# A ring of eight gathered rows beside the attention heads, and the buffers that make room for it

## The reference, cut to what matters

```
def peer_block(xb):                                   # 128 frames
    q = (xb @ w_pq).reshape(t, PEER_HEADS, 2, PEER_HALF)
    s = einsum('thpd,phkd->thpk', q, sub_keys)        # 2 x 128 scores, 8 heads
    top_s, top_i = top_k(s, 16)
    best_s, best_j = top_k(all 256 sums, 16)          # 16 experts per frame and head
    g = softmax(best_s)
    h = einsum('td,thkd->thk', xb, u_emb[expert])
    act = g * gelu(h)
    return einsum('thk,thkd->td', act, v_emb[expert])
x = x + peer(rms_norm(x, g_ffn));  y = rms_norm(x, g_final)
```

## Time and profile before

| what | value |
|---|---|
| median of 3 runs | 3593.12 us (3592.84 to 3595.46) |
| the profiled execution's own time | 3593.41 us |
| its span, first to last instruction | 3591.7 us |
| granted TensorE clock, mean | 0.848 |
| first gather issued | 484.85 us |
| last gather issued | 3564.17 us |

### The profile page before, as it was taken

The page is one execution under the profiler, slowest core; times in us unless marked ns, Lnnn a source line. Parts: engine busy times, 40 slices in busy tenths (PEclk is TensorE's granted clock), DMA queues, the critical chain, the costliest instruction groups (busy, mean ns, idle before and its releaser), DMA issues. The chain is left out here.

```text
span 3591.7 us, 41643 instructions
## 1 busy us (share of the span) xinstructions
PE 2535.7 (71%) x13407; PEld 1076.0 (30%) x13407; DVE 2442.1 (68%) x6857; ACT 1020.4 (28%) x2925; POOL 1418.8 (40%) x1266
## 2 busy tenths in 40 slices
PE   5999867666866677667666866687667666666654
PEld 3444533222322233223322332233223222222211
DVE  2888666667666666776667667666667666666774
ACT  2333322222222222222322222323332222222321
POOL 0332434434444443444434443434344434344443
PEclk9999889887888898888888988887888878888866
DMA  7112369999999999999999999999999999999997
GB/s 251 47 50 70 98 230 381 382 386 383 396 391 384 380 386 379 380 379 385 393 380 382 388 379 388 374 385 376 385 370 401 378 374 369 344 385 371 365 371 297
DMA packets 219401, 1220.43 MB, mean 340 GB/s; under 512 B 33091, under 2 KB 60419, under 8 KB 79942
## 3 DMA queue, kind: packets, MB, share of 16 engines
q0 software_dynamic: 156672, 1140.92, 81.4%
q1 hardware_dynamic: 62533, 77.09, 6.6%
HBM read 1199.51 MB, written 18.42 MB: 339 GB/s over the span
## 5 line engine op out<-in xcount | busy, mean ns | idle before, releaser
L1374 PE MATMUL ps<-uv_rows,diag 64*64 64x512 f32 x8704 | 1381.8, 761 | 967.7 <-ACT diag L1619 966.8
L1270 POOL DMA_INDIRECT uv_rows<-in_uv_emb,experts x1088 | 1255.6, 1154 | 1823.9 <-PE ps L1374 1536.1
L1832 DVE CUSTOM_DVE_ANT_0 uv_rows<-uv_rows,handed 128x1024 f32<-128x1024 f32 x1088 | 1331.9, 1224 | 862.6 <-DMA uv_rows<-in_uv_emb,experts 856.7
L1374 PEld LDWEIGHTS ps<-uv_rows,diag 64*64 64x64 f32 x8704 | 329.1, 157 | 1655.0 <-ACT diag L1619 1221.8
L1611 ACT ACTIVATE gelu_c<-dots 128x2 f32<-128x2 f32 x544 | 110.8, 204 | 1880.4 <-DVE dots L1832 1880.0
L1619 ACT ACTIVATE diag<-ident_twice,act_c 128x64 f32<-128x64 f32 x1088 | 319.1, 340 | 286.4 <-DVE act_c L1849 285.8
L1334 PE MATMUL ps<-w_pq_sb,xnT_c 128*128 128x256 f32 x1152 | 349.1, 434 | 0.7 <-ACT xnT_c L1580 0.7
L1334 PEld LDWEIGHTS ps<-w_pq_sb,xnT_c 128*128 128x128 f32 x1152 | 224.7, 212 | 260.6 <-issue 236.0
L568 PE MATMUL ps<-w_in_sb,w_out_sb 128*128 128x512 f32 (+1 forms) x656 | 243.3, 526 | 16.8 <-ACT w_out_sb L454 16.8
L626 DVE SCALAR_TENSOR_TENSOR handed<-w_out_sb,tapsT,handed 128x128 f32<-128x128 f32 x960 | 252.8, 343 | 0.0
L389 POOL TENSOR_TENSOR rstd_a<-ms_a,neg_half 128x1 f32<-128x1 f32 x9 | 82.5, 9166 | 205.2 <-ACT ms_a L435 205.2
(11 more groups left out here) (244 smaller groups left out, 2127.1 us busy)
## 6 DMA issues: line engine op xcount, KB each, us to landing
uv_rows<-in_uv_emb,experts POOLq DMA_INDIRECT x1088, 9.0
w_in_sb<-in_w_in SPq DMA_DIRECT2D x4, 2048.0 KB, 11.7
w_pq_sb<-in_w_pq SPq DMA_DIRECT2D x8, 1024.0 KB, 12.2
w_out_sb<-in_x_prompt SPq DMA_DIRECT2D x8, 512.0 KB, 3.9
handed<-in_x_prompt SPq DMA_DIRECT2D x8, 512.0 KB, 3.8
w_out_sb<-in_w_out SPq DMA_DIRECT2D x1, 4096.0 KB, 19.3
out<-handed SPq DMA_DIRECT2D x8, 512.0 KB, 9.3
keys_turned<-handed SPq DMA_DIRECT2D x10, 260.0 KB
```

Of the source, the lines that this page charges most:

```text
L1270: nc.gpsimd.indirect_dma_start(out=rows[:, m % RING, :], out_offset=None, in_=d.uv_emb[0], in_offset=bass.IndirectOffsetOnAxis(ap=experts[ ...
L1374: ins = pe.matmul(ps[dst, 2 * x + half, :], diag[src, (m + i) % DIAGS, :], rows[src, (m + i) % RING, cols], start=first, stop=last)
L1832: nc.vector.tensor_tensor_reduce(out=row, in0=row, in1=xn[:, block_of(n) % 2, :], scale=1.0, scalar=0.0, op0=ALU.mult, op1=ALU.add, accum_ ...
```

## The change

The ring has eight rows instead of six. Each row takes 8 KB in every partition, and these buffers are given up or made smaller for it:

- `DIAGS` is 6 instead of 8.
- `q` and `qT` share one buffer, so that ACT waits with the next query until the scores are made. `half_s` has one buffer for two, so that the copy of the scores waits until the choice before has read its own.
- `gf` is gone. `gm` holds the chunks of both gains, and a new `final_gains` makes the final gain in PSUM (bank `X_`, half by half, in steps 9 and 13 of a block's first item; for the sample frames in two banks after the last item). `normalise` works on halves, in steps 12 and 15, from PSUM. `y_ready` counts two for a block, and `store` and `project` wait for both.
- The sample frames' convolution `y_s` lives in phase B alone. SP stores it to HBM at that phase's end and waits for it. Phase C loads it as it loads that of the other blocks.
- `probsT` holds one piece of up to 512 keys for two. The values are weighed piece by piece (`weigh_head_values` in step 3 and step 5, `pv_piece` in place of `pv_psum`), and the second piece is copied out when the first was weighed. `q_pair` is the first 128 columns of `probsT`, so that the query rows are loaded after step 5 of the item before their use, and no longer two pairs ahead.
- `heads_o` is the first half of `catT`, from the third head on. The first two heads of a block go to a small buffer `first_o`, as `catT` is still read by the projection then. `z` shares `conv_in`. Nine small columns are one tile.

```
-        RING = 6
-        DIAGS = 8
+        RING = 8
+        DIAGS = 6
-        qT = sb("qT_c", [P, 2, P])
-        half_s = sb("half_scores", [P, 2, 2, s.NKEYS])
+        qT = q[:, :].rearrange("p (a t) -> p a t", a=2)
+        half_s = sb("half_scores", [P, 2, s.NKEYS])
-        gm = sb("g_ffn_chunks", [s.DCH, P])
-        gf = sb("g_final_rows", [P, s.D])
+        gm = sb("gain_chunks", [2 * s.DCH, P])
-        q_pair = sb("pair_queries", [P, 2 * s.HD])
-        probsT = sb("head_probsT", [P, 2, BANK])
-        heads_o = sb("head_outputs", [P, s.DA])
+        probsT = sb("head_probsT", [P, BANK])
+        q_pair = probsT[:, 0:2 * s.HD]
+        first_o = sb("first_outputs", [P, P])
+        heads_o = catT[:, 0:s.CCH, :].rearrange("p c t -> p (c t)")
...
-        z = sb("conv_rows", [P, s.DC])
+        z = conv_in[:, :, :].rearrange("p c t -> p (c t)")
...
 # phase B, SP, at its end
+            sp.wait_ge(taps_done, 1)
+            sp.dma_start(d.conv[s.NB, :, :, 0:s.TS], y_s[:, :, :]).then_inc(y_kept, 16)
+            sp.wait_ge(y_kept, 16)
...
 # phase C, SP
-                sp.wait_ge(y_ready, b + 1)
+                sp.wait_ge(y_ready, 2 * (b + 1))
...
-            sp.dma_start(gf[:, :], d.g_final.partition_broadcast(P)).then_inc(gains_here, 16)
+            sp.dma_start(gm[s.DCH:2 * s.DCH, :], d.g_final.rearrange("(c p) -> c p", p=P)).then_inc(gains_here, 16)
-            sp.wait_ge(qT_h_psum, 1)
-            load_query_rows(1)
             for n in range(HEADS):
                 if 2 <= n < ITEMS and n % 2 == 0:
-                    sp.wait_ge(pv_psum, n)
+                    sp.wait_ge(pv_piece, pieces_before(n))
                     load_values(n // 2)
+                if n % 2 == 1 and n + 1 < ITEMS:
+                    sp.wait_ge(pv_piece, pieces_before(n))
+                    load_query_rows((n + 1) // 2)
...
-                if n % 2 == 1 and (n + 1) // 2 + 1 < ITEMS // 2:
-                    sp.wait_ge(qT_h_psum, (n + 1) // 2 + 1)
-                    load_query_rows((n + 1) // 2 + 1)
...
 # phase C, PE: in project, i == 0
+                    if p > 1:
+                        pe.wait_ge(y_ready, 2 * (p - 1))
...
+            def final_gains(b, half):
+                pe.wait_ge(gains_here, 32)
+                if b < s.NB:
+                    pe.wait_ge(y_ready, 2 * b + half)
+                bank = X_ if b < s.NB else X_ + half
+                for x in range(4):
+                    row = s.DCH + 4 * half + x
+                    ins = pe.matmul(ps[:, bank, x * P:(x + 1) * P],
+                                    g.ident[0:2 * s.DCH, row:row + 1].broadcast_to([2 * s.DCH, P]), gm[:, :], start=True, stop=True)
+                ins.then_inc(final_psum, 1)
...
+            def weigh_head_values(i, piece):
+                lo, hi = pieces_of(i)[piece]
+                pe.wait_ge(turned_ready, pieces_before(i) + piece + 1)
...
+                for x in range(lo, hi, P):
+                    ins = pe.matmul(ps[:, S_, O_AT:O_AT + s.HD], probsT[:, x - lo:x - lo + P],
+                                    v_pair[:, x // P, (h % 2) * s.HD:(h % 2 + 1) * s.HD], start=(x == 0), stop=(last and x == hi - P))
+                ins.then_inc(pv_piece, 1)
...
                     if k == 3 and len(pieces_of(i)) == 2:
+                        weigh_head_values(i, 0)
                         turn_head_probs(i, 1)
...
+                    if n >= PH and n % PH == 0 and n <= PROMPT and k in (9, 13):
+                        final_gains(block_of(n) - 1, (k - 9) // 4)
...
 # phase C, ACT
+                if r > 0:
+                    act.wait_ge(s_psum, r)          # query_out
...
-                if r >= 2:
-                    act.wait_ge(s_used, r - 1)
+                if r > 0:
+                    act.wait_ge(s_used, r)          # scores_out
...
-                if i > 0:
-                    act.wait_ge(pv_psum, i)
+                if i > 0 or piece:
+                    act.wait_ge(pv_piece, pieces_before(i) + piece)   # head_probs_out
...
+                if h == 2:
+                    act.wait_ge(x1_psum, 2 * (i // s.H + 1))          # head_output
+                dst = first_o if h < 2 else heads_o
...
 # phase C, DVE
-            def normalise(b):
+            def normalise(b, half):
...
+                dve.wait_ge(final_psum, 2 * b + half + 1)
+                nc.vector.scalar_tensor_tensor(out=x1[0:r, b % 2, cols], in0=x1[0:r, b % 2, cols], scalar=rms[0:r, 2:3],
+                                               in1=ps[0:r, bank, :], op0=ALU.mult, op1=ALU.mult).then_inc(y_ready, 1)
```

More of the change, by code:

```diff
@@ L749, in tap @@
                                                    in1=c.tapsT[:, :, j:j + 1].broadcast_to([P, s.CCH, s.TS]), op=ALU.mult))
-                before = g.b_dw.unsqueeze(2).broadcast_to([P, s.CCH, s.TS]) if j == 0 else g.y_s[:, :, :]
-                ins = nc.gpsimd.tensor_tensor(out=g.y_s[:, :, :], in0=tapped[:, :, :], in1=before, op=ALU.add)
+                before = g.b_dw.unsqueeze(2).broadcast_to([P, s.CCH, s.TS]) if j == 0 else y_s[:, :, :]
+                ins = nc.gpsimd.tensor_tensor(out=y_s[:, :, :], in0=tapped[:, :, :], in1=before, op=ALU.add)
                 if j + 1 < s.TAPS:
@@ L1222, in load_query_rows @@
                 b, h = item_of(2 * pair)
-                sp.dma_start(q_pair[:, :], d.q[b, :, h * s.HD:(h + 2) * s.HD]).then_inc(q_here, 16)
+                sp.dma_start(q_pair, d.q[b, :, h * s.HD:(h + 2) * s.HD]).then_inc(q_here, 16)
             def load_conv(b):
-                sp.dma_start(conv_in[:, :, :], d.conv[b]).then_inc(conv_here, 16)
+                t = P if b < s.NB else s.TS
+                sp.dma_start(conv_in[:, :, 0:t], d.conv[b, :, :, 0:t]).then_inc(conv_here, 16)
             load_query_rows(0)
@@ L1422, in turn_conv @@
                 pe.wait_ge(piece_read, pieces_before(s.H * i + 3))
-                if b < s.NB:
-                    pe.wait_ge(conv_here, 16 * (i + 1))
+                pe.wait_ge(conv_here, 16 * (i + 1))
+                t = P if b < s.NB else s.TS
                 for x in range(s.CCH):
[L1426 to L1429, removed]
+                    ins = pe.transpose(ps[0:t, B_, x * P:(x + 1) * P], conv_in[:, x, 0:t], g.ident[:, :])
                 ins.then_inc(y_psum, 1)
@@ L1445, in turn_outputs @@
                 for x in range(s.CCH):
-                    ins = pe.transpose(ps[:, B_, x * P:(x + 1) * P], heads_o[:, x * P:(x + 1) * P], g.ident[:, :])
+                    ins = pe.transpose(ps[:, B_, x * P:(x + 1) * P], first_o[:, :] if x == 0 else heads_o[:, x * P:(x + 1) * P],
+                                       g.ident[:, :])
                 ins.then_inc(oT_psum, 1)
+            def final_gains(b, half):
[6 more added lines that the diff above has]
+                    ins = pe.matmul(ps[:, bank, x * P:(x + 1) * P],
+                                    g.ident[0:2 * s.DCH, row:row + 1].broadcast_to([2 * s.DCH, P]), gm[:, :], start=True, stop=True)
+                ins.then_inc(final_psum, 1)
             def head_scores(i, piece):
@@ L1492, in weigh_head_values @@
                 pe.wait_ge(s_out, issued.scores)
[L1493 to L1499, removed]
+                last = hi == keys_of(i)
+                if last:
+                    issued.values += 1
+                for x in range(lo, hi, P):
+                    ins = pe.matmul(ps[:, S_, O_AT:O_AT + s.HD], probsT[:, x - lo:x - lo + P],
+                                    v_pair[:, x // P, (h % 2) * s.HD:(h % 2 + 1) * s.HD], start=(x == 0), stop=(last and x == hi - P))
+                ins.then_inc(pv_piece, 1)
             def head_step(n, k):
@@ L1572, in _ @@
                             turn_query(routed[1])
+                    if n >= PH and n % PH == 0 and n <= PROMPT and k in (9, 13):
+                        final_gains(block_of(n) - 1, (k - 9) // 4)
                     head_step(n, k)
+            for half in range(2):
+                final_gains(s.NB, half)
         @block.scalar
@@ L1638, in conv_rows_out @@
                 act.wait_ge(y_psum, i + 1)
-                if i > 0:
-                    act.wait_ge(zT_psum, i)
                 own = slice(0, P if FIRST + i < s.NB else s.TS)
-                nc.scalar.copy(z[own, :], ps[own, B_, :]).then_inc(y_out, 1)
+                nc.scalar.copy(z[own], ps[own, B_, :]).then_inc(y_out, 1)
             def conv_scaled(i):
@@ L1658, in head_probs_out @@
                 act.wait_ge(turned_psum, pieces_before(i) + piece + 1)
-                if i > 0:
-                    act.wait_ge(pv_psum, i)
-                nc.scalar.copy(probsT[:, piece, 0:hi - lo], ps[:, B_, 0:hi - lo]).then_inc(turned_ready, 1)
+                if i > 0 or piece:
+                    act.wait_ge(pv_piece, pieces_before(i) + piece)
+                nc.scalar.copy(probsT[:, 0:hi - lo], ps[:, B_, 0:hi - lo]).then_inc(turned_ready, 1)
             def head_output(i):
                 _, h = item_of(i)
-                at = O_AT
```

(16 more changed lines are left out.)

38 lines of the change are left out of this document (15 added, 23 removed).

## The result

The changed kernel takes 3393.24 us (median of 4 runs, 3392.87 to 3393.65), the kernel before 3594.29 us beside it: the ratio is 0.9433, 95% interval 0.941 to 0.9455. That is 201 us less where 112 were forecast, and under the range of 3435 to 3565. The profiled execution of the changed kernel has a span of 3391.9 us.

The account below looks back on a forecast made before the run. The prediction took phase C to be bound by its gathers, with too few in the DMA at a time. From 3593.4 us it took 115 for the ring and added 2.7 and 0.2: 3481 us, range 3430 to 3534.

Parts of the forecast that it names:

- What bounds the kernel: Phase C runs at the pace of its gathered rows, in a loop of 17.4 us for six rows; depth is short.
- The ring's term: Two more ring rows in phase C raise 380 GB/s to 395 over 1155 MB: 115 us less.
- The burst: At the first gathers, six issued before one was used moved 426 and 433 GB/s; one or two out, 341.
- The third reading: 504 stretches of 5 us sorted by gathers out: 354 GB/s with 2, 390 with 3, 404 with 4.
- The part outside the DMA stays 8.0 us: Of a ring turn in phase C, 8.0 us stay outside the DMA, so both added rows go into it.
- The convolution's store: End of phase B: the new store stands behind POOL's last tap, 2.7 us on the path, between 2 and 5.
- Smaller diagonals: ACT's diagonals of a pair wait until PE has weighed the pair three before: no cost.
- The final gain: PE's added matmuls and DVE's half reads: hidden, 0.2 us on the path; 21 or 16 us if not covered.
- SP's queue: Query rows loaded after step 5 for step 15: 27 us against a landing of 6.8 that may grow by 5; nothing.
- The rival of the late small loads: The deeper queue delays SP's query rows past step 15, so PE waits; 3643 us at landings of 33 us; chance 0.05.
- Share only: Rival: the DMA's rate while busy doesn't rise, only its idle tenths go: 3550 us (3534 to 3575); chance 0.24.
- no gain: Rival: something that depth doesn't touch sets 380 GB/s, such as memory or POOL's descriptors: 3596 us; chance 0.06.

Follow-up runs that it names:

- e4: Kernel before, ring of six, PE weighing only the first half of the v columns (except a block's first pair): 3457.95 us, ratio 0.9585.
- e5: Changed kernel with six ring rows and no attention heads, their loads or the convolution's in phase C: 3576.31 us, ratio 0.993 to the kernel before.
- e2: Changed kernel with seven ring rows instead of eight: 3404.29 us, ratio 0.9437 to the kernel before.
- e7: Changed kernel with ten ring rows and no attention heads, their loads or the convolution's in phase C: 3294.0 us, ratio 0.9146 to the kernel before.
- e9: Changed kernel with five more of POOL's convolution taps made before its wait for the norm's sum in phase B: 3385.57 us, ratio 0.9405 to the kernel before.
- e1: Changed kernel with six ring rows, all its other edits kept: 3616.17 us, ratio 1.0032 to the kernel before.
- e3: Changed kernel with the expert's number made of the second key alone, so gathers read within 1 MB: 3393.29 us, ratio 0.9402 to the kernel before.
- e8: Changed kernel, ring of eight, with the second half of PE's weighing left out: 3390.0 us, ratio 0.9413 to the kernel before.

## Why the prediction was wrong, point by point

- *What bounds the kernel.* Right: a loop of fixed latencies around a DMA that is busy by share and short of work by bytes. e4 and e5 show it from two sides, at six rows.
- *The ring's term.* The mechanism was right, and the size was off; this is the step that failed. The prediction had 404 GB/s for 4 gathers out in its own classes, and took 395 for about 5 out, for three reasons: short stretches overshoot a little, POOL was idle in the burst, and attention's keys and values come in smaller packets. Measured are 407, so that the term is 202 us and not 115. With 404 it would have been 181. Attention's packets were already in the 404: in the 41 stretches of that class the queues other than the gathers' moved 17 GB/s (12 in the class of 3). POOL's issuing was in it too, if for 29% of the time only, and costs nothing that can be seen: in the changed kernel's class of 4 POOL issued for 51% of the time, at 405 GB/s. The overshoot of the share to 1.005 is no error of short stretches either; the DMA of the changed kernel reads 1.01 over 2820 us.
- *The burst.* Of the three readings by which the DMA was not full, the second was wrong. Counted as in the classes, the stretch from 500.0 us with 433 GB/s had first 3 and then 2 gathers out, and the one from 507.5 us with 341 had 3 or 4. Six were issued by 492.3 us, but by 500.9 us DVE had begun four dots:

```profile
500.86 1.22 DVE L1832 CUSTOM_DVE_ANT_0 uv_rows<-uv_rows,handed 128x1024 f32<-128x1024 f32 x1
...
506.06 1.16 POOL L1270 DMA_INDIRECT uv_rows<-in_uv_emb,experts  x1 [0.98 <-PE ps L1374]
507.52 0.93 POOL L1270 DMA_INDIRECT uv_rows<-in_uv_emb,experts  x1 [0.30 <-issue]
...
509.63 1.23 DVE L1832 CUSTOM_DVE_ANT_0 uv_rows<-uv_rows,handed 128x1024 f32<-128x1024 f32 x1 [2.38 <-DMA uv_rows<-in_uv_emb,experts]
```

  So the burst is no sign that more gathers out move more, and 433 was no rate of six. The third reading, by classes, was sound as far as it went, and the runs with more rows bear the conclusion out.
- *How the depth acts.* The prediction read the classes as a slope, more out, more rate. e2 and e7 show that it levels off: seven rows are nearly enough, and ten bring nothing over eight. A reader of the classes could have suspected it from the shares: 0.945 with 2 out, 0.992 with 3, 1.005 with 4. Why 3 out move less in the kernel before than in e2, and 2 or 3 moved 433 GB/s in the burst, stays open.
- *The part outside the DMA stays 8.0 us.* Right: 7.9 us. From a pair's first dot to the gather into its slot the median is 8.2 us before and 7.9 after. Landings of 13.8 us were forecast, 13.2 measured.
- *DVE's waits for DMA* near 730 us were forecast, 642 measured: the same term.
- *The convolution's store.* 2.7 us forecast; POOL's idle at the border of the phases grew from 0.34 to 2.74 us, and phase C began 2.0 us later. Its place on the path was right, as e9 shows.
- *Smaller diagonals.* Nothing, right in the changed kernel: ACT's diagonals wait for PE 0.9 us in all, in 3 waits.
- *The final gain.* The halves take 742 ns each, and DVE's wait for PE's matmuls is 3.0 us in 2 waits, where up to 16 were allowed for. On the path after the last item are 1.40 us for 1.28 (0.2 were forecast). Right.
- *SP's queue.* The query rows land in 7.2 us in the median and 8.3 at most (6.8 before). No wait of PE for them is in the trace. The allowance that they might grow by the gathers' 5 us was far too large: with two gathers more out, 64 KB on SP's queue took 0.4 us longer. The rival of the late small loads had no ground.
- *Other edits together.* "Nothing" was forecast beside the store. e1 has 12 us (1 to 21) at six rows, which may be more than the store. At eight rows no run tells them apart.
- *Noise.* The prediction said that 7 us can be told from no change. For the kernel before that was too fine: beside e1 its 13 runs spread from 3595 to 3624. The 201 us are far clear of it.
- *Share only* and *no gain* are out: the share rose from 0.98 to 1.01 and the rate by 7%. The Trainium skill's 358 GB/s (DMA: Bandwidth & Descriptors, "Where 436 GB/s comes from") doesn't bind here; the trace has 407 over 2820 us. Its 425 GB/s for 16 MB, by which 3275 us were worked out, is 4% above what this kernel reached; without the heads it reached 415.

## What to carry to other kernels

A DMA share of 0.98 was not a full DMA here. Look at the bytes, sort short stretches by how many transfers are out, and before taking anything off the rate of the fullest class, look whether its stretches already contain what one would take off. For these gathers of 1 MB the depth was enough when the fewest out, not the mean, was about three. Below that, one row was worth some 200 us, and a microsecond less between landing and release, on an engine that is idle for 29% of the span, 150. Beyond it the next row gave 11 us, two more gave nothing, and the shorter release 3. Two quick trials tell the side: take a bystander's traffic away (a gain of far less than its bytes, or a rate that falls, means latency-bound), and shorten the release.

## What the runs showed of the hardware that was not expected

- A gather of 128 rows of 8 KB lands in 5.5 us at best in the kernel before, while without the heads one passes every 2.55 us at eight rows (3263.8 - 491.0 us for 1087 gathers). An estimate from these two: 5.5 / 2.55, so that two to three in flight cover one's latency.
- Rows scattered over 134 MB and rows within 1 MB come at the same 407 GB/s (e3).
- The 16 matmuls that weigh a pair took 1.99 us at a granted clock of 1.00 and 3.61 us at 0.54, within one stretch of 100 us. They stand in the part of a turn outside the DMA.
- TensorE's granted clock between 520 and 3230 us was 0.87 of full speed in the mean in the changed kernel and 0.70 in e8, where half of the weighing matmuls are left out. So more of that stretch was granted 1.2 GHz and less 2.4 GHz, with PE busy for 1724 us instead of 1955, and the time changed by 3 us of 3393.
